# Gate and up of a feed-forward as seven block products of half size, and the feed-forward in thirds

## The reference

```python
def swiglu(h, w_gate, w_up, w_down):
    return (jax.nn.silu(h @ w_gate) * (h @ w_up)) @ w_down

for i in range(DEPTH):
    xp = xp + 0.5 * swiglu(rmsnorm(xp, ffn_norm[i, 0]), ffn_w_gate[i, 0], ffn_w_up[i, 0], ffn_w_down[i, 0])
    hp = rmsnorm(xp, mix_norm[i])
    ...
    xp = xp + yp
    xp = xp + 0.5 * swiglu(rmsnorm(xp, ffn_norm[i, 1]), ffn_w_gate[i, 1], ffn_w_up[i, 1], ffn_w_down[i, 1])
```

## Time and profile before

| | us |
|---|---|
| median of three timed runs | 2314.74 |
| their lowest and highest | 2313.84, 2318.51 |
| the profiled execution, first to last instruction (span) | 2312.3 |
| a feed-forward (ffn2): gate and up | 267.5 |
| ffn2: down | 131.1 |

### The profile page before, as it was taken

The page is one execution under the profiler, slowest core; times in us unless marked ns, Lnnn a source line. Parts: engine busy times, 40 slices in busy tenths (PEclk is TensorE's granted clock), DMA queues, the critical chain, the costliest instruction groups (busy, mean ns, idle before and its releaser), DMA issues.

```text
span 2312.3 us, 39554 instructions
## 1 busy us (share of the span) xinstructions
PE 2240.9 (97%) x14674; PEld 2015.9 (87%) x14691; DVE 1146.9 (50%) x1863; ACT 404.4 (17%) x826; POOL 1029.1 (45%) x625
## 2 busy tenths in 40 slices
PE   7999999999989899999999999999999999999997
PEld 6999999949666588999999999999997789999997
DVE  4545422488785446555421555542266465455311
ACT  3001000131554312010000110100015320100002
POOL 4555455414101035555555555555541055555552
PEclk9999999999998999999999999999999899999998
DMA  4435344636003523333323333332351033333231
GB/s 124 103 73 118 77 118 124 122 66 148 11 1 113 154 68 78 82 82 82 82 80 92 83 82 82 82 82 81 94 153 25 1 83 83 82 82 81 80 85 59
DMA packets 378041, 196.32 MB, mean 85 GB/s; under 512 B 66531, under 2 KB 374476, under 8 KB 377932
## 3 DMA queue, kind: packets, MB, share of 16 engines
q1 hardware_dynamic: 366108, 180.79, 31.6%
q10 hardware_dynamic: 11552, 13.71, 1.9%
q0 software_dynamic: 288, 0.56, 0.2%
HBM read 192.23 MB, written 11.64 MB: 88 GB/s over the span
## 4 chain that ended last, share of the span: by engine, by line
PE 62%; DVE 2%; ACT 0%; issue 0%; DVEq 0%; ACTq 0%
PE psum L608 17%; PE psum L611 11%; PE psum L609 11%; PE psum L607 11%; PE psum L610 9%; DVE XS L1570 1%; PE psum L842 1%; PE psum L858 1%; PE psum L872 1%; PE psum L838 1%; DVE squares L1603 0%; PE psum L1019 0%; PE psum L1020 0%; PE psum L628 0%; PE psum L693 0%
## 5 line engine op out<-in xcount | busy, mean ns | idle before, releaser
L545 POOL CAST WSP<-WST 128x1024 fp32r<-128x1024 f32 (+1 forms) x305 | 308.8, 1013 | 1218.2 <-PE psum L611 1007.9
L547 POOL TENSOR_TENSOR WSP<-WST,WSP 128x1024 fp32r<-128x1024 f32 (+1 forms) x305 | 708.0, 2321 | 24.4
L608 PE MATMUL psum<-XS,WSP 128*128 128x512 f32 x1672 | 658.3, 394 | 0.0
L607 PE MATMUL psum<-XS,WSP 128*128 128x320 f32 x1672 | 520.5, 311 | 10.0 <-DVE XS L1570 4.3
L611 PE MATMUL psum<-XS,WSP 128*128 128x320 f32 x1672 | 522.3, 312 | 0.0
L609 PE MATMUL psum<-XS,WSP 128*128 128x320 f32 x1672 | 519.0, 310 | 0.0
L610 PE MATMUL psum<-XS,WSP 128*128 128x256 f32 x1672 | 473.7, 283 | 0.0
L610 PEld LDWEIGHTS psum<-XS,WSP 128*128 128x128 f32 x1672 | 314.7, 188 | 71.4
L607 PEld LDWEIGHTS psum<-XS,WSP 128*128 128x128 f32 x1672 | 321.4, 192 | 12.2 <-DVE XS L1570 5.2
L611 PEld LDWEIGHTS psum<-XS,WSP 128*128 128x128 f32 x1672 | 321.2, 192 | 0.0
L608 PEld LDWEIGHTS psum<-XS,WSP 128*128 128x128 f32 x1672 | 314.3, 188 | 0.4
(11 more groups left out here) (320 smaller groups left out, 2561.6 us busy)
## 6 DMA issues: line engine op xcount, KB each, us to landing
WST<-in_ffn_w_gate SPq DMA_DIRECT2D x168, 256.0 KB, 3.9
WST<-in_ffn_w_up SPq DMA_DIRECT2D x168, 256.0 KB, 3.9
WST<-in_ffn_w_down SPq DMA_DIRECT2D x192, 224.0 KB, 3.5
WST<-in_a_w_in SPq DMA_DIRECT2D x28, 256.0 KB, 4.3
kv0A<-in_cache_kv SPq DMA_DIRECT2D x48, 128.0 KB, 2.3
kv2A<-in_cache_kv SPq DMA_DIRECT2D x48, 128.0 KB, 2.3
WST<-in_b_w_in SPq DMA_DIRECT2D x20, 256.0 KB, 4.2
kscr<-in_cache_idx SPq DMA_DIRECT2D x128, 32.0 KB, 2.0
```

The source lines that it names most:

```text
L545: nc.gpsimd.tensor_copy(WSP[s][:, 0, 0:width], WST[s][:, 0:width]).then_inc(w_hi, 1)
L547: nc.gpsimd.tensor_tensor(WSP[s][:, 1, 0:width], WST[s][:, 0:width], WSP[s][:, 0, 0:width].bitcast(F32), ALU.subtract).then_inc(w_split, 1)
L607: mm(front, high, x[:, 0, 0:FRONT], start=first, stop=False)
L608: mm(split, high, x[:, :, FRONT:TOK], start=first, stop=False)
```

## The change

The width of a feed-forward is now worked in three thirds of seven blocks. For each block p, gate (G) and up (U) are made together. The inputs are split into even and odd blocks of features (e, o), the tokens into a first and a second half of 288 (1, 2). That is a 2 x 2 by 2 x 2 block product, made with seven products instead of eight by sums of blocks ahead and behind: with S1 = U_e + U_o, S2 = -S1 - G_e, S4 = G_o - S2, S3 = G_e + U_e for the weights and four sums of tokens for the activations (XT; P5 takes e1 - e2, P6, P7 and P4 take it with the odd blocks). Each product is four pairs of blocks of three matmuls of 288 columns:

```diff
+PRODUCTS = ("P1", "P5", "P6", "P3", "P2", "P7", "P4")
+FIRST = ("P5", "P1", "P2", "P6", "P3", "P7")
+REST = ("P1", "P5", "P4", "P6", "P3", "P2", "P7")
+AHEAD = 3
+XTRA_HALVES = 5
+XTRA_RAW = 1
...
+            def product(name, p, prod, out, first=False, last=False, ready=lambda k: None):
+                high, low = weight_parts((name, p, prod))
+                for k in range(KP):
+                    c = slice(k * P, (k + 1) * P)
+                    ready(k)
+                    mm(out, high[:, c], operand(prod, 0, k), start=first and k == 0, stop=False, skip_group_check=True)
+                    mm(out, high[:, c], operand(prod, 1, k), start=False, stop=False, skip_group_check=True)
+                    ins = mm(out, low[:, c], operand(prod, 0, k), start=False, stop=last and k == KP - 1, skip_group_check=True)
+                ins.then_inc(w_used, 1)
```

On PE the first block of a third has the order FIRST, the others REST, where P4 is that of the block before. The waits of `p1` to `p7` (shortened):

```diff
+            def p1(name, p):
+                if n > 1:
+                    pe.wait_ge(hidden_set, 2 * (n - 1))
...
+                    if p == 0:
+                        pe.wait_ge(xl_done, 8 * e + 2 * k + 1)
+            def p5(name, p):
...
+                if p == 0:
+                    pe.wait_ge(x_upd, 8 * e + 7)
+                    pe.wait_ge(tl_pool, 2 * (4 * i + KP - 1) + 1)
+            def p4(name, p):
+                pe.wait_ge(up_sum, n + 1)
+                pe.wait_ge(pool_set, POOLED[name, p, "P4"])
```

Behind the last block of a third comes `down(name, q)`, seven `mm3` for each of the 8 d, added into X at once (three times a feed-forward). The Python loops are written out; there is no `Fori`. The high parts of the seven products are made by ACT, the low parts of five and the sums S1 and S3 by POOL, S2 and S4 (in PSUM) and the low parts of P6 and P3 by DVE. In the order of each engine:

```diff
+            def pair(name, p, behind=lambda n: None):          # POOL
+                if is_first(p):
+                    sum_up(name, p)                             # S1
+                behind(0)
+                low_of_raw(name, p, "P1")
+                low_of_sum(name, p, "P5")
+                behind(1)
+                sum_first(name, p)                              # S3
+                low_of_raw(name, p, "P2")
+                behind(2)
+                low_of_sum(name, p, "P7")
+                behind(3)
+                if not is_last(p):
+                    sum_up(name, p + 1)
+                low_of_raw(name, p, "P4")
...
+                    for p in range(q * DB + 1, (q + 1) * DB):  # ACT, ffn
+                        next_high(p, "P1")
+                        shot_1(name, p)
+                        next_high(p, "P5")
+                        shot_5(name, p)
+                        next_high(p, "P6")
+                        next_high(p, "P3")
+                        shot_2(name, p)
+                        hidden_high(name, p - 1)
+                        next_high(p, "P2")
+                        next_high(p, "P7")
+                        silu(name, p)
+                        next_high(p, "P4")
...
+                    sums(name, p + 1)                           # DVE, ffn
+                    if p == 0:
+                        rms(e - 1)
+                        dve.wait_ge(t_sum, 4 * 4 * (i + 1))
+                    lows_of_sums(name, p + 1)
+                    gate_first(name, p)
+                    gate_second(name, p)
+                    gate_scaled(name, p)
+                    for p in range(q * DB + 1, (q + 1) * DB):
+                        up_second(name, p - 1)
+                        if not is_last(p):
+                            sums(name, p + 1)
+                            lows_of_sums(name, p + 1)
+                        hidden(name, p - 1)
+                        hidden_low(name, p - 1)
+                        gate_second(name, p)
+                        gate_first(name, p)
+                        gate_scaled(name, p)
```

(In the code the comments are not there.) `next_high(p, ...)` is the high part for block p + 1. In the first block of a third ACT's order is `shot_5`, P1, `shot_1`, P5, (root), P6, `shot_2`, P3, P2, silu, P7, P4. `shot_1`, `shot_5` and `shot_2` copy an unfinished accumulator of 288 columns to SBUF, as the products share accumulators. `sums` is:

```diff
+            def sums(name, p):
+                gate = (name, p, "gate")
+                dve.wait_ge(pool_set, POOLED[name, p, "S1"])
+                dve.wait_ge(stage_in[RAW[gate]], LANDED[gate])
...
+                stt(by_pair(S2), by_pair(S1), -1.0, raw_part(gate, 0), ALU.mult, ALU.subtract).then_inc(sums_set, 1)
+                dve.wait_ge(sums_set, SUMMED[name, p, "S2"])
+                tt(by_pair(S4), raw_part(gate, 1), by_pair(S2), ALU.subtract).then_inc(sums_set, 1)
```

The sums of tokens are made during the stage before: ACT scales X by the gain (`scaled`), POOL makes `near_sum` and `far_sums`, ACT their high parts, POOL and DVE their low parts. POOL's order for the first block (`start`) puts them between the weights:

```diff
+                def behind(n):
+                    if n == 0:
+                        token_low(i, 1, 1)
+                        near_sum(i, 2)
+                    elif n == 1:
+                        token_low(i, 2, 0)
+                        far_sums(i, 2)
+                        near_sum(i, 3)
+                        token_low(i, 2, 1)
+                    elif n == 2:
+                        token_low(i, 3, 0)
+                        far_sums(i, 3)
+                    else:
+                        token_low(i, 3, 1)
+                pair(name, 0, behind)
```

More of the change, by code:

```diff
@@ L65 @@
 RING = 3
-DB = NF // RING
-GU_CHUNKS, DN_CHUNKS = 2 * NF, ND * RING
 A_CHUNKS, B_CHUNKS = 1 + IH // 2 + 2 + GRP, 2 + GRP
[L71 to L81, removed]
+FFNS = ("ffn0", "ffn1", "ffn2", "ffn3")
@@ new lines, with raw_order @@
+DONE = {key: n + 1 for n, key in enumerate(weight_order())}
+PLACE, EARLIER = weight_places()
+def raw_order():
+    order = []
+    for name in STAGES:
+        if name not in FFNS:
+            order += [(name, c) for c in range(CHUNKS_OF[name])]
+            continue
+        for q in range(THIRDS):
+            for p in range(q * DB, (q + 1) * DB):
+                order += [(name, p, "up"), (name, p, "gate")]
+            order += [(name, "down", q, d) for d in range(ND)]
+    return order
@@ new lines, in bass_hybrid_step, with half_tile, weight_parts @@
+        MS = {L: {k: sem(k + L) for k in both + only[L] if k not in absent[L]} for L in "AB"}
+        low_slots = [(A_CHUNKS - KVH - 1 + n) % RING for n in range(KVH)]
+        raws = WST + WSTX
+        def half_tile(h):
+            if h == 2 * RING + XTRA_HALVES - 1 and XTRA_HALVES % 2:
+                return WSH
+            return (WSP + WSX)[h // 2][:, :, h % 2 * KP * P:(h % 2 + 1) * KP * P]
+        def weight_parts(key):
+            w = half_tile(PLACE[key][0])
+            return w[:, 0, :], w[:, 1, :]
@@ L431, in parts @@
                         return [(d[n * HD:(n + 1) * HD], v[n, :, :, t * P:(t + 1) * P]) for n in range(KVH)]
[L432 removed]
+                    load((name, t), parts)
             def pages_of(b):
@@ L463, in kist @@
                 if b < 2:
-                    sp.wait_ge(w_used, over("ffn0"))
+                    sp.wait_ge(w_used, DONE["ffn0", "down", THIRDS - 1, ND - 1])
                 else:
@@ L502, in _ @@
             for c, parts in enumerate(todo):
-                chunk(n0 + c, 0, 0, parts)
+                load(("inA", c), parts)
                 if 2 <= c < 6:
@@ L516, in _ @@
             for c, parts in enumerate(todo):
-                chunk(at["inB"][0] + c, 0, 0, parts)
+                load(("inB", c), parts)
             project_out("outB", io["b_w_out"][0], 0, ND)
@@ new lines, in ffn @@
+            def ffn(name, after=None):
+                for q in range(THIRDS):
+                    for p in range(q * DB, (q + 1) * DB):
+                        if p:
+                            pair(name, p)
+                    for d in range(AHEAD):
+                        down(name, q, d)
+                    if q == THIRDS - 1 and after:
+                        start(after, lambda d: down(name, q, d))
+                    else:
+                        for d in range(AHEAD, ND):
+                            down(name, q, d)
```

913 lines of the change are left out of this document (666 added, 247 removed).

## The result

The changed kernel takes 2342.25 us (median of 4 runs, 2338.89 to 2349.45) against 2314.39 for the kernel before beside it: a ratio of 1.0123, 95% interval 1.0103 to 1.0143. It is slower by 1.2%; 2277 was predicted, and 2342 lies outside the range too.

A forecast was written before the change was run, and what follows sets the result against it. TensorE, busy 97% of the span, was taken as the bound, so only fewer columns or added waits could move the time. Saving 124 less 16, 51, 16 and 3 gave 38 us: 2277 us, range 2208 to 2335.

The forecast's parts named there:

- SyncE's queue: Loads in ffn0 landing late behind the 21.3 us page gather: four of seven cost 4 us each, 16 us lost.
- the starts: Start of each feed-forward, where TensorE waits for token sums and statistics: 51 us lost (18 in ffn0, 12, 9, 12).
- costs put at nothing: Written-out loops, constants for registers and hidden VectorE updates of X counted as free; down blocks kept at 0.780 us.
- the ring: Chain of waits across GpSimd, VectorE and ScalarE from pair to pair: 11.45 us against TensorE's 11.21, 16 us lost.
- the tail: At the kernel's end, y's rows wait for X in steps of 5.5 instead of 16 us: 3 us lost.
- The matmuls: Gate and up: 84 matmuls of 288 columns at 0.1335 us save 1.48 us a pair, 124 us over 84 pairs.
- Rival (c): A 288-column matmul costs what 320 columns do, 0.142 us; saving only 64 us, time 2321 us; chance 0.12.
- Rival (b): The chain of waits between engines sets the pace at 12.8 us a pair: 65 us lost, 2342 us; chance 0.17.
- T - 4.3: Last even row of X ready 4.3 us before T, the last down block of the stage before a feed-forward.
- T + 2.7: Token sum for P5 ready 2.7 us after T, the last down block of the stage before a feed-forward.

The follow-up runs named there:

- both: Changed kernel with ffn0's page gather issued in pieces of four pages and three orders changed at the feed-forward starts: 2292.79 us, ratio 0.9903 to the kernel before.
- cut: "both" with ScalarE's high part for P2 of the next pair put ahead of the hidden product's high part: 2288.05 us, ratio 0.9881 to the kernel before.

## Why the prediction was wrong

The sum was 124 - 16 - 51 - 16 - 3 = 38 us won; the spans lost 35. Of these 73 us SyncE's queue makes up 29, the starts 19 and costs put at nothing 27, while the ring and the tail were put 3 too high each; the gain against which they stand was right.

**The matmuls, 124: right.** 7056 x 0.133 us against 1344 blocks of 0.793 are 127; by the mean inside a third, hand-overs between products counted (0.1334), 124. Rival (c) is out.

**The ring, 16: the chain is there, its price is not.** It takes 11.2 us for 11.45 and so stands level with TensorE's 11.17: opening it took 0.2 us off a third. Rival (b) named the time, 2342, but with a ring of 12.8 us, so that was luck. It is luck too that 13 us came in this term's place. TensorE lost 0.7 to 1.0 us a third ahead of P1 of the third pair, 6 us in the later thirds, which opening the ring did not give back. What was not foreseen is one event in two of 84 pairs, where S2 took 5.54 us and TensorE lost 3.6, 7 together; whether the three other runs of this kernel had such events is not recorded. GpSimd and VectorE, after:

```profile
1619.63 1.31 POOL L760 TENSOR_TENSOR WSP<-WSTX,WSP 128x512 fp32r<-128x512 f32 x1
1620.89 1.29 POOL L760 TENSOR_TENSOR WSP<-WST,WSP 128x512 fp32r<-128x512 f32 x1
1622.14 1.28 POOL L769 TENSOR_TENSOR WSP<-S,WSP 128x512 fp32r<-128x512 f32 x1
1623.38 1.31 POOL L751 TENSOR_TENSOR S<-WST 128x512 f32<-128x512 f32 x1
```

```profile
1619.71 5.54 DVE L2163 SCALAR_TENSOR_TENSOR psum<-S,WST 128x512 f32<-128x512 f32 x1 [1.50 <-POOL S L741]
```

S2 began 0.08 us behind the first of four GpSimd instructions and ended 0.56 behind the last: three more began and ended while it ran, so it was passed over three times, which the prediction ruled out from the earlier trace rows. The Trainium skill, "SBUF — State Buffer", section "Who interferes with whom", lets the first issued hold the ports and the other wait it out; the usual 1.78 us agrees, this case does not, as three of the four started after S2.

**SyncE's queue, 16: the step that failed.** The prediction had four of seven waits at 4 us. Five came, 3.8 to 8.0 us ahead of P6 and in pair 20 3.6 more ahead of P3, 34 us together; with the 1.2 GHz matmuls behind each (1.7 to 2.6 us) it is 45, and taking the cause away gave 40. The prediction set the 22.4 us that two pairs of raw tiles last against the gather's 21.3 and let a load land 3 to 7 us late. But a tile is not free until its pair's last low part: the queue stands idle some 9 us between two pairs' loads and the gather holds it for 20, so that a load came some 10 us late. And on ScalarE, and on VectorE as well, work that does not need the load stood behind work that does. The upper end of 28 was too low as well.

**The starts, 51: mis-sized, 70.** P5 began 17.6 us later in ffn0, not 9, and waited 5.5 to 7.5 in the others. The first thirds took 7 (ffn0, without the gather), 15, 8 and 15 us more than a later third's 77.5; the starts before, some 10 in all, go off. The failed link is the row of X: the prediction had the last even row, which P5's sum of tokens needs, in X at T - 4.3, 1316.5 us in ffn2, as VectorE's rows were to be hidden ("8 x 1.2 us in 5.5 us steps"). TensorE ended that row at 1311.9, and VectorE had it in X at 1320.85. Beside GpSimd's sums VectorE's instructions are longer (a square sum 1.36 us for 0.75), and ScalarE's queue stood idle 5.82 us for S1 and 3.21 for a sum of tokens (ScalarE, VectorE, then GpSimd, after):

```profile
1308.49 0.63 ACT L1638 ACTIVATE WSH<-S 128x512 fp32r<-128x512 f32 x1 [5.82 <-POOL S L741]
...
1321.26 0.78 ACT L1666 ACTIVATE gs<-X,gains 128x576 f32<-128x576 f32 x1 [3.21 <-POOL tsum L805]
```

```profile
1317.63 1.36 DVE L2262 TENSOR_TENSOR squares<-squares 128x576 f32<-128x576 f32 x1
...
1319.65 0.74 DVE L2269 SCALAR_TENSOR_TENSOR X<-psum,X 128x576 f32<-128x576 f32 x1
1320.43 0.42 DVE L2271 SCALAR_TENSOR_TENSOR X<-psum,X 128x256 f32<-128x256 f32 x1
```

```profile
1327.30 0.80 POOL L810 TENSOR_TENSOR XT<-tsum,XT 128x288 fp32r<-128x288 f32 x1
```

From there on it went about as counted, to GpSimd's low part at 1328.1; the prediction's T + 2.7 for P5 became T + 7.5, and 4.4 of these 4.8 us are that row's. In ffn0 too the last row of X came late, at 41.4 us and not 30.3, with ScalarE idle 2.48 us for S1 and 2.96 for a sum of tokens.

**Costs put at nothing.** Down blocks took 0.793 for 0.780 us, 672 x 0.013 = 9 us. The last down third of ffn1 waited 3.5 us for accumulators that late rows of X held. The mixers came out some 15 us longer (12 and 3), beside the waits counted as starts. The trace places some 9 of it: 4.0 us in the first two blocks of the mixer behind ffn0, where TensorE waits 2.87 us for GpSimd's low part of the first chunk and goes on at 1.2 GHz, 1.8 more than before ahead of the gathered keys, and 1.9 in each mixer's output projection, where it waits for late rows of X; no run isolates any of them. The clock was not in the sum: a wait of several microseconds was followed by matmuls 0.24 apart, 1.7 to 2.6 us more behind each gather and 2.6 behind P5 of ffn2 (counted above where the wait is). The tail's 3 us did not show (14.8 us behind the last block, 15.4 before).

In the spans: -124 + 13 + 45 + 70 + 9 + 3.5 + 15 is 31.5 of the 35 measured.

## What to carry to other kernels

When TensorE gets faster, list everything that was sized to its old pace, and for a shared queue compare the longest block in it with the time for which it stands idle between two issues, not with how long the buffers last. Look behind a late load for work that does not need it but stands in line behind work that does, on every engine. A sum moved from TensorE to GpSimd is cheap inside a stage and dear at its start, where the same engines make the input; and a chain of hand-overs as long as TensorE's own work costs nothing until the next saving, so measure it by cutting TensorE's work short.

## What the runs showed of the hardware

VectorE can be passed over by several GpSimd instructions in a row (S2 took 5.54 us for 0.69 in two of 84 pairs here, and in one or two pairs of three other kernels). Changing one instruction's place on ScalarE took the average S2 from 1.56 to 0.94 us ("both" to "cut"): it began inside a GpSimd instruction in 68 of 84 pairs before and in 20 after, and takes 1.7 to 1.8 us on average where it does, 0.69 where it does not.
